# Experts in rounds of three on column quarters of the array, the fourth quarter for more places of the largest

## What is computed

```python
def hier_moe(h, router_g, router_g_b, router_e, router_e_b, w_gate, w_up, w_down):
    # the best of 4 groups for each token, then the best 2 of its 8 experts;
    # gates: their softmax, times the group's probability
    ...
    for gi in range(N_EXPERT_GROUPS):
        hid = jax.nn.silu(jnp.einsum('td,edf->tef', xt, w_gate[gi])) * jnp.einsum('td,edf->tef', xt, w_up[gi])
        hid = hid * gates[:, gi, :, None].astype(hid.dtype)
        out = out + jnp.einsum('tef,efd->td', hid, w_down[gi]).astype(f32)
```

## Time and profile before

| | us |
|---|---|
| median of 3 runs | 2693.57 (2691.61 to 2694.58) |
| profiled execution | 2689.26 |
| its span, first to last instruction | 2687.5 |
| PE busy | 2408.3 (90%) |
| DVE busy | 899.7 (33%) |
| first layers of the experts (L2130), PE busy | 453.6 |
| second layers (L2147) | 230.8 |
| scatter (L2160) | 237.0 |

### The profile page before, as it was taken

One profiled execution on the slowest core, in us unless ns is written; L12 is line 12 of the kernel. 1 busy time (PEld: TensorE's weight loads), 2 busy tenths in 40 slices (PEclk: granted clock), 3 DMA queues, 4 the chain that ended last, 5 costly groups with the idle time before them and its releaser, 6 DMA issues. The chain is left out here.

```text
span 2687.5 us, 35679 instructions
## 1 busy us (share of the span) xinstructions
PE 2408.3 (90%) x15097; PEld 1324.2 (49%) x15097; DVE 899.7 (33%) x1809; ACT 407.8 (15%) x769; POOL 100.3 (4%) x186
## 2 busy tenths in 40 slices
PE   5989997799989999879997999779997999779996
PEld 3668886433338766743333554343333554334332
DVE  5876775521123111532112441221113440321112
ACT  0033332010000001410000232100001132100001
POOL 0000000010000000001000000001000000001000
PEclk7989998799999999979998999889998999889998
DMA  9700001759995663126997434327997434326995
GB/s 370 291 1 3 4 4 58 319 210 421 421 416 196 229 216 146 53 76 287 421 421 294 156 121 177 114 97 293 422 421 292 146 122 175 126 94 276 421 421 227
DMA packets 138898, 601.87 MB, mean 224 GB/s; under 512 B 33832, under 2 KB 36968, under 8 KB 83952
## 3 DMA queue, kind: packets, MB, share of 16 engines
q1 hardware_dynamic: 126480, 591.64, 56.1%
q10 hardware_dynamic: 12000, 7.88, 1.1%
q0 software_dynamic: 256, 0.02, 0.0%
HBM read 598.43 MB, written 1.05 MB: 223 GB/s over the span
## 5 line engine op out<-in xcount | busy, mean ns | idle before, releaser
L2130 PE MATMUL ps<-arena,region 128*64 128x512 f32 x2048 | 453.6, 595 | 5.3 <-POOL region L2273 5.3
L2727 PE MATMUL ps<-arena,x_features 128*128 128x512 f32 x704 | 321.3, 600 | 3.9 <-PEq L678 3.9
L2130 PEld LDWEIGHTS ps<-arena,region 128*64 128x64 f32 x2048 | 141.1, 137 | 272.5 <-issue 265.7
L2160 PE MATMUL ps<-region 128*128 128x512 f32 x512 | 237.0, 605 | 0.0
L2147 PE MATMUL ps<-arena,region 128*64 128x512 f32 x1024 | 230.8, 592 | 2.1 <-DVE region L2248 2.1
L2255 DVE COPY region<-ps 128x512 f32<-128x512 f32 x64 | 44.4, 693 | 554.6 <-PE ps L2147 554.6
L341 PE MATMUL ps<-arena,region 128*128 128x512 f32 x480 | 213.2, 605 | 11.0 <-PEq L678 7.9
L2727 PEld LDWEIGHTS ps<-arena,x_features 128*128 128x128 f32 x704 | 127.7, 191 | 135.7 <-issue 133.5
L371 PE MATMUL ps<-x_features,arena 128*128 128x256 f32 x768 | 168.4, 382 | 2.5 <-PEq L678 2.5
L2197 ACT ACTIVATE region<-ps 128x512 f32<-128x512 f32 x64 | 38.3, 599 | 833.4 <-PE ps L2147 833.4
L2160 PEld LDWEIGHTS ps<-region 128*128 128x128 f32 x512 | 91.7, 189 | 144.2 <-issue 144.2
(11 more groups left out here) (412 smaller groups left out, 2424.9 us busy)
## 6 DMA issues: line engine op xcount, KB each, us to landing
arena<-in_moe_w_gate SPq DMA_DIRECT2D x64, 1024.0 KB, 11.9
arena<-in_moe_w_up SPq DMA_DIRECT2D x64, 1024.0 KB, 13.8
arena<-in_moe_w_down SPq DMA_DIRECT2D x64, 1024.0 KB, 17.3
arena<-in_w_exp_gate SPq DMA_DIRECT2D x64, 1024.0 KB, 11.1
arena<-in_w_exp_up SPq DMA_DIRECT2D x64, 1024.0 KB, 13.2
arena<-in_w_exp_down SPq DMA_DIRECT2D x64, 1024.0 KB, 16.7
arena<-in_ada_w SPq DMA_DIRECT2D x48, 1024.0 KB, 13.7
arena<-in_w_in SPq DMA_DIRECT2D x40, 1024.0 KB, 5.0
```

The lines of the kernel that those rows point to most:

```text
L2130: mm = pe.matmul(v3(k.ps[e * CAP:(e + 1) * CAP, 6, :], 2, F), xe[:, q % 2, s, e], w, start=(s == 0), stop=(s == K8 - 1), skip_group_check= ...
L2160: pe.matmul(k.ps[:, 2 * tile + h, :], gatedT[:, q % 2, tile * P:(tile + 1) * P], out[:, h * HALF:(h + 1) * HALF], start=False, stop=True, ...
L2727: mm = pe.matmul(k.ps[:, 2 * (j % 2) + tile, :], x, row[:, 0:HALF], start=(s_ == 0), stop=(s_ == K8 - 1))
```

## The change

Three experts make a round, each on a quarter of the array's columns with 32 places (`CAP`). Round q has the experts q, q + 11 and q + 22; eleven rounds, of which the last has two experts. The first quarter takes the places 32 to 63 of the round's largest expert. Which it is comes out of the routing (`pick`), and TensorE reads the number of its slots (`k.spare`) into a register; the products of this quarter address the weights by it. For that the gate and up units now have the slots 0 to 7 as four pairs, the down units the slots 8 to 11 as four single ones, each taken in turn, and the down units are counted by a semaphore of their own (`second_layers_used`).

The first round's tokens don't come from the sorted ones: `take_tokens` multiplies the tokens with the round's own selection (`slots`). The sorting follows behind the first round's first layer, on two banks of PSUM in place of four. The zero products stand in the routing block now. The routing makes the places for four quarters with 33 columns (32 experts and an empty one), with one running sum in place of five doubling steps. The general path is taken when an expert has more than its 32 places, or 64 for the largest of its round. The diff's core:

```diff
-PAIRS = EXPERTS // 2
-CAP = P // 2
+
+ROUNDS, WIDE = 11, 4
+CAP = P // WIDE
+EX = (WIDE - 1) * ROUNDS
...
+        def first(q, ws=range(WIDE - 1)):
+            for e, w in ((w * ROUNDS + q, w) for w in ws):
+                if e < EXPERTS:
+                    for half, v in enumerate((g, u)):
+                        units.append(v[e])
+                        tags.append((f"{'gu'[half]}{layer}", e))
+                        places.append(("first", (WIDE - 1) * q + w, half))
+
+        def second(q, ws=range(WIDE - 1)):
+            for e, w in ((w * ROUNDS + q, w) for w in ws):
+                if e < EXPERTS:
+                    units.append(d[e])
+                    tags.append((f"d{layer}", e))
+                    places.append(("second", (WIDE - 1) * q + w, 0))
+
+        first(0)
+        first(1, (0,))
+        second(0)
+        second(1, (0,))
+        first(1, (1, 2))
+        first(2)
+        second(1, (1, 2))
+        for q in range(2, ROUNDS):
+            if q + 1 < ROUNDS:
+                first(q + 1)
+            second(q)
+        assert len(units) == 3 * EXPERTS
+        return units, tags, places
 
     def conditions(i, spans):
...
+
+            layer = int(name[3:])
+            if layer not in k.turn:
+                k.turn[layer] = min(range(4), key=lambda m: k.last[2 * m])
+            for kind, m, half in tags[1]:
+                at = (m + k.turn[layer]) % 4
+                if kind == "first":
+                    take(2 * at + half, k.used, start + 2 * m + half + 1)
+                else:
+                    take(8 + at, k.used_second, EXPERTS * layer + m + 1)
+            continue
         for u in range(len(k.slots), n, 2):
-            pair = min(ring[::2], key=lambda at: k.last[at])
...
-                k.rounds[at] += 1
...
         sp.dma_start(dst, src).then_inc(k.landed[at], 16)
     k.issued = max(k.issued, min(upto, len(k.plan)))
...
-                    mm_ = pe.matmul(k.ps[:, 3, n * EXPERTS:(n + 1) * EXPERTS], w, chosen[:, tile], start=(m == 0),
...
+                pe.matmul(k.ps[:, b, :], zero, k.places[:, :], start=True, stop=True)
 
         @block.scalar
...
 
+            vec.wait_ge(k.pool_done.sem, k.pool_done.at(1))
+            link(vec.tensor_scalar(turn_.bitcast(I32), turn_.bitcast(I32), 3, None, ALU.bitwise_and))
+            link(vec.tensor_copy(turn_, turn_.bitcast(I32)))
+            link(vec.tensor_copy(order_, order_.bitcast(I32)))
...
+            link(vec.tensor_copy(rank, v3(k.ps[:, 4, 0:TILES * EX], TILES, EX)))
+            link(vec.tensor_copy(totals, k.ps[:, 4, TILES * EX:(TILES + 1) * EX]))
+            link(vec.tensor_tensor_scan(summed, ones[:, 0:EX], totals, 0.0, MUL, ADD))
...
+            link(vec.scalar_tensor_tensor(out=above, in0=totals, scalar=float(WIDE), in1=order_, op0=MUL, op1=ADD))
+            link(vec.tensor_reduce(largest, by_round(above), X, MAX))
+            link(vec.tensor_tensor(by_round(pick), by_round(above),
+                                   largest.rearrange("p (q a) -> p q a", a=1).to_broadcast([P, ROUNDS, WIDE - 1]), ALU.is_equal))
+            link(vec.tensor_tensor(above, turn_, pick, MUL))
+            link(vec.tensor_reduce(largest, by_round(above), X, ADD))
+            link(vec.tensor_copy(k.spare, largest))
+            link(vec.tensor_copy(starts[:, :, 1:WIDE], by_round(first_place)))
+            link(vec.scalar_tensor_tensor(out=above, in0=first_place, scalar=float(CAP), in1=pick, op0=ADD, op1=MUL))
+            link(vec.tensor_reduce(starts[:, :, 0], by_round(above), X, ADD))
+            link(vec.tensor_copy(k.firsts, starts.rearrange("p q w -> p (q w)")))
+            link(vec.tensor_tensor(other, gates, each(pick), MUL))
+            link(vec.tensor_reduce(k.gate[:, :, :, 0], by_round(other), X, ADD))
+            link(vec.tensor_tensor(other, rank, chosen, ADD))
+            link(vec.tensor_copy(k.key[:, :, :, 1:WIDE], by_round(other)))
+            link(vec.scalar_tensor_tensor(out=other, in0=other, scalar=float(CAP), in1=each(pick), op0=SUB, op1=MUL))
+            link(vec.tensor_reduce(k.key[:, :, :, 0], by_round(other), X, ADD))
...
+            link(vec.tensor_tensor(over, rank, each(limit), ALU.is_ge))
+            link(vec.tensor_tensor(k.over.rearrange("p e t -> p t e"), over[:, :, 0:EXPERTS], gates[:, :, 0:EXPERTS], MUL))
...
+
+
+                wait_pair(pe, k.slots_built, 0)
+                for s in range(K8):
+                    for tile in range(TILES):
+                        mm = pe.matmul(k.ps[:, 4 + s // 4, (s % 4) * P:(s % 4 + 1) * P], tokens(tile, s),
+                                       slots[:, tile].rearrange("p w n -> p (w n)"), start=(tile == 0), stop=(tile == 1))
+                    if s % 4 == 3:
+                        mm.then_inc(k.taken.sem, 1)
...
+            pairs = k.arena[:, 0:8 * SLOT].rearrange("p (m x) -> p m x", m=4)
+            singles = k.arena[:, 8 * SLOT:12 * SLOT].rearrange("p (m x) -> p m x", m=4)
+            spare = {}
+
             def first_layer(q):
 
-                pe.wait_ge(k.window_ready.sem, k.window_ready.at(2 * (q + 1)))
+                spare[q] = pe.value_load(k.spare[0:1, q:q + 1], min_val=0, max_val=3)
                 if q:
+                    pe.wait_ge(k.window_ready.sem, k.window_ready.at(WIDE * q))
                     wait_pair(pe, k.hidden_ready, q - 1)
-                for m in range(4):
-                    wait_slot(pe, gate_at(q) + m)
+                else:
+                    pe.wait_ge(k.taken_act.sem, k.taken_act.at(1))
+                    pe.wait_ge(k.taken_vec.sem, k.taken_vec.at(1))
+                wait_slots(pe, "gu", q)
+                es = experts_of(q)
                 for s in range(K8):
-                    for e in range(2):
-                        w = v3(slot(gate_at(q) + 2 * e, 2), 2, SLOT)[:, :, s * F:(s + 1) * F]
-                        mm = pe.matmul(v3(k.ps[e * CAP:(e + 1) * CAP, 6, :], 2, F), xe[:, q % 2, s, e], w,
-                                       start=(s == 0), stop=(s == K8 - 1), skip_group_check=True)
-                        if s == K8 - 1:
-                            mm.then_inc(k.used, 2)
+                    for w in range(WIDE):
+                        both = (pairs[:, bass.ds(spare[q], 1)].rearrange("p a (z x) -> p (a z) x", z=2) if w == 0 else
+                                v3(slot("g", es[min(w, len(es)) - 1], 2), 2, SLOT))
+                        mm = pe.matmul(v3(k.ps[w * CAP:(w + 1) * CAP, 6, :], 2, F), xe[:, q % 2, s, w],
+                                       both[:, :, s * F:(s + 1) * F], start=(s == 0), stop=(s == K8 - 1), skip_group_check=True)
+                mm.then_inc(k.used, 2 * len(es))
 
             def second_layer(q):
 
...
+                es = experts_of(q)
                 for h in range(2):
                     for r in range(2):
-                        for e in range(2):
-                            w = v3(slot(down_at(q) + e), 2, D)
-                            mm = pe.matmul(k.ps[e * CAP:(e + 1) * CAP, 4 + h, :], hidT[:, r, e * CAP:(e + 1) * CAP],
-                                           w[:, r, h * HALF:(h + 1) * HALF], start=(r == 0), stop=(r == 1),
+                        for w in range(WIDE):
+                            both = (singles[:, bass.ds(spare[q], 1)].rearrange("p a (z x) -> p (a z) x", z=2) if w == 0 else
...
             overflow(pe, general)
+            take_tokens()
+            turn(-1, False, True)
+            first_layer(0)
             order_tokens()
             pe.wait_ge(k.sorted_act.sem, k.sorted_act.at(4))
             pe.wait_ge(k.sorted_vec.sem, k.sorted_vec.at(4))
-            turn(-1, False, True)
-            first_layer(0)
-            for q in range(PAIRS):
-                turn(q, True, q + 1 < PAIRS)
-                if q + 1 < PAIRS:
+            for q in range(ROUNDS):
+                turn(q, True, q + 1 < ROUNDS)
+                if q + 1 < ROUNDS:
                     first_layer(q + 1)
                 second_layer(q)
-                scatter(q)
+                mm = scatter(q)
+            mm.then_inc(k.used, EXPERTS)
```

215 lines of the change are left out of this document (120 added, 95 removed).

## The result

Before 2693.05 us (2691.61 to 2694.58, 4 runs), after **2730.73 us** (2723.59 to 2737.98, 4 runs): ratio 1.0139, 95% interval 1.0124 to 1.0155. The change makes the kernel 1.4% slower. The forecast was 2671, range 2654 to 2700. The runs of after lie 14 us apart, those of before 3.

The account below looks back on a forecast made before the run. TensorE bound the kernel, with the DMA 3% slower right behind. Per layer -14.1 + 2.8 + (240.0 - 234.4) = -5.7 us, four layers -22.8: 2689.3 to 2666.5, plus 4.3 for the runs' median: 2671 us, range 2654 to 2700.

Parts of the forecast that it names:

- Front: Start of expert block to first expert product: 8.7 us in place of 22.8, 14.1 us less per layer.
- Router to counting: VectorE's four operations ahead of the logits and GpSimd's five beside router products: nothing, or up to 1 us in second half.
- Routing chain: VectorE after the counting products: 33 chained operations in 7.6 us, where 24 took 4.81; +2.8 us per layer.
- Does the DMA run without a gap? ... 2.9 us in hand: Steady rounds: next first layer ends at T+19.5, 2.9 us less than the DMA's 22.4, so transfers go on without gap.
- hidden in the middle of a layer: Mid-layer first layers beginning at low clock take 9.3 us in place of 7.1, covered by the 2.9 us in hand.
- 238.3: Expert part from first expert product to last scatter, before the clock term: 238.3 us, where before had 234.4.
- The clock term of 1.7 us a layer: Low clock not hidden in first and last rounds: 1.7 us added per layer, bounds 0 and 5.7, giving 240.0.
- rival B: Slower by the clock: first layers from round 2 on at half clock throughout, 14.2 us; 151 us more, 2822; chance 0.10.
- Rival A: No change: a gap in the DMA in the rounds eats the front's 14 us; 2690; chance 0.10.
- What comes after a layer: nothing lost: Behind a layer: next weights land from 7 us before its end, next products start 16.6 us after it; nothing lost.
- Tail of a layer: Layer end: last but two units landed by 222.4, last unit at 230.9, last second layer and scatter end at 238.3 us.

Follow-up runs that it names:

- e4_half2: Changed kernel, but each expert-layer unit after the first in its slot is loaded by half only (result not the reference's); 2518.3 us.
- e1_warm: Changed kernel plus six unread 128x512 products on TensorE in each round from round 1 on, between transposes and next first layer; 2724.3 us.
- e13_warm_cap: Changed kernel plus added unread products ahead of the first layers of rounds 2 to 9, and SyncE capped at four next-stage units; 2703.7 us.
- e2_cap: Changed kernel, but SyncE issues at most four units of the next stage in the expert block, the others in the next block; 2725.1 us.
- e12_rows_ahead: Changed kernel with every round's tokens from rows of neighbouring features, second layer before next first layer, sorting's routing operations dropped, SyncE issues uncapped; 2663.2 us.
- e6_take: Changed kernel, but every round's tokens are taken from the rows by 16 products and the sorting is gone; 2716.1 us.
- e3_rounds: Changed kernel, but round 0's tokens come from the sorted places again, with the sorting ahead of the first round; 2781.9 us.
- e5_warm2: Changed kernel plus six unread products on TensorE ahead of the first layers of rounds 3 to 8 alone; 2716.8 us.

## Why the prediction was wrong, step by step

- **Front**: 14.1 less a layer forecast. `take_tokens` took 6.76 (forecast 6.0); 13.1 less a layer in the mean, fewer in layers 2 and 3 (front 10.8 and 11.2 us against 9.9 and 8.3 in the first two), where its weight loads are strided. Right but for that size.
- **Router to counting**: nothing forecast, up to 1 us in the second half; in layers 2 and 3 it was 1.2 and 0.9. In layers 0 and 1 it takes 12.4 to 13.9 in all runs, whatever the kernel.
- **Routing chain**: +2.8 forecast, +3.2 measured. Right.
- **"Does the DMA run without a gap? ... 2.9 us in hand"**: this is the step that failed. The mechanism was set up rightly (the loop from the landing of four units through the first layer to the next issue), and both its terms were too small. The landing I took at 4.9 us from an idle queue and called it the worst case; in the loops with a first layer over 9.4 us it was 4.8 to 7.6. The first layer I took at 7.1, or 9.3 with the clock; it was 8.4 to 10.0. The loop needed up to 17.55 us where 14.9 were free. So the low clock was not "hidden in the middle of a layer": 8.3 us lost in the first expert layer, and at the restart behind round 0 another 3.3 (38.9 us after the first expert product, forecast 35.6). 238.3 + 8.3 + 3.3 and 0.2 in the tail make 250.1, the measured length of the first expert layer; in the mean of the four it is 238.3 + 8.8 + 2.4 + 0.2 = 249.7. e4_half2 shows the DMA as the bound, e1_warm that the gaps close with a clock kept up, e13_warm_cap the worth: 5.5 us a layer. Neither term would have done it alone: with first layers of 7.07 us the next unit landed 2.6 us after the one before, and with the landing at 4.9 the long loops would have fitted.
- **The clock term of 1.7 us a layer** was mis-sized for the same reason: I charged it to the first and last rounds alone. TensorE's clock stood at its lower level for 6.8 us in most rounds, of which the products at 740.72 had 5.7 (to 746.4), where I took 4.4. That is how the Trainium skill's "TensorE: Matmul & The Clock Gate", on HAM oscillation, tells it: each burst behind a wait for the DMA starts low. By rival B, low to the end, a round would be 26.6; by the rows it was 23.1. B was nearer in kind than in size.
- **Rival A** (a gap in the DMA) described what happened, at the right place; I priced it at no change because I let it take only the gain.
- **"What comes after a layer: nothing lost"**: wrong by 14 us between layers. I looked at the first products of the next stage and not at what the barrier waits for. (I also misread the rows: in before the next stage's first unit lands 11 us before the end of layer 0, not 7; in after 4.5.) With a queue backed up, one issue on SyncE takes 2.4 to 3.0 us and holds the barrier behind layer 0 (7.1 us lost; e2_cap: 5.3 back; e12_rows_ahead: residual 1.1 us after the layer's end with a short queue, after has 8.7). Ahead of two routers SyncE's issues of down units cost 1.3 and 1.1. The rest, in the main 3.1 us of clock behind layer 1, was read from the traces only, and its cause is open; 2.8 us ahead of layer 0 lie within what this stretch shows across the runs (520.0 to 522.6).
- **Tail of a layer**: from the last but two landing to the end 15.9 forecast, 16.1 measured. Right.

Sum: 39.6 + 17.0 + 2.4 + 1.6 + 4.1 = 64.7 us, against 65.0 between the profiled execution (2731.5) and its forecast (2666.5).

## What to carry to other kernels

When a change makes the DMA the bound and lets the compute engine wait, price the loop "landing, burst, issue, landing" with the burst at the low clock and the landing at its slowest row, not with the best of each; a margin of 2.9 us on 22.4 was none. A gap in work is best filled with work that something needs: the sorting held in one place put the first layer of round 1 off by 5 us (24.6 us behind that of round 0, against 19.6 in e6_take), while the same tokens taken in each round's wait left TensorE still waiting 2 to 4 us a round where the weight loads are contiguous. Filler that nobody needs has to stop where the wait stops: in the last round of e1_warm it cost 8 us. Before a barrier look at every engine, and at the queue that only issues.

## What the runs showed of the hardware that I had not expected

- From issue to landing of a 1.05 MB unit, in after and the five runs e1_warm, e2_cap, e3_rounds, e5_warm2 and e13_warm_cap: 4.7 to 6.1 us with the queue idle, 4.8 to 7.6 when it was issued 2.0 to 2.5 us before the unit ahead of it landed. The first of the 16 engines was done after 3.9 to 4.8 and 4.0 to 4.5 us; the last was late. Issued 5.0 us or more before that landing, it landed 2.4 to 3.1 us after it, about a unit's own 2.5. Why the last engine is late when the issue comes 2.0 to 2.5 us ahead is open.
- Weight loads of 128x128 float32 with a stride of eight: 337 ns, against 192. A product with 128 columns pays for it (7.94 us for 32 instructions against 3.84), one with 512 does not.
- Six products that take 5.32 us together, in a wait of 6 to 8 us, kept the clock at its upper level in about two rounds of three; in the others 3.4 us at the lower level were left.
